# The down projection of a decoder step, with each 128-row product made as two 64-row products in two banks

## The reference

```python
def conv_ffn(x, g, w_up_l, cw, w_down_l, prev):
    u = rmsnorm(x, g) @ w_up_l
    u, new = causal_dwconv(u, prev, cw)
    a, b = jnp.split(u, 2, axis=-1)
    return (jax.nn.silu(a) * b) @ w_down_l, new      # added to x by the caller
```

## Time and profile before

| what | us |
|---|---|
| median of 3 runs | 956.81 (956.18 to 958.14) |
| the profiled execution's own time | 958.85 |
| its span, first to last instruction | 957.2 |

### The profile page before, as it was taken

The page is one execution under the profiler, slowest core; times in us unless marked ns, Lnnn a source line. Parts: engine busy times, 40 slices in busy tenths (PEclk is TensorE's granted clock), DMA queues, the critical chain, the costliest instruction groups (busy, mean ns, idle before and its releaser), DMA issues.

```text
span 957.2 us, 17553 instructions
## 1 busy us (share of the span) xinstructions
PE 915.7 (96%) x6566; PEld 860.2 (90%) x6566; DVE 627.3 (66%) x1280; ACT 446.6 (47%) x752; POOL 283.6 (30%) x565
## 2 busy tenths in 40 slices
PE   5889999998999999999989999999899999999996
PEld 4889998996779999999989999899677999999996
DVE  4667863654368999984555787355435899998442
ACT  4453541444447555553344254235444655555342
POOL 1412310252004666630042231005210465563001
PEclk9989998899789999999999999889978999999999
DMA  8654631196235566555556554108641655564432
GB/s 255 175 140 135 182 94 46 56 244 181 73 88 150 160 176 168 156 174 169 157 149 168 170 172 122 45 21 225 184 126 46 175 167 153 167 177 158 160 124 67
DMA packets 209406, 137.69 MB, mean 144 GB/s; under 512 B 23475, under 2 KB 202203, under 8 KB 209323
## 3 DMA queue, kind: packets, MB, share of 16 engines
q1 hardware_dynamic: 199904, 111.11, 41.1%
q0 software_dynamic: 8288, 22.85, 8.3%
q10 hardware_dynamic: 1131, 2.62, 0.8%
HBM read 131.11 MB, written 5.44 MB: 143 GB/s over the span
## 4 chain that ended last, share of the span: by engine, by line
PE 91%; DVE 4%; DMA 2%; ACT 1%; issue 1%; DVEq 1%; ACTq 0%; SPq 0%
PE banks L1213 22%; PE banks L1215 21%; PE banks L1214 21%; PE banks L1391 3%; PE banks L1473 2%; PE banks L1356 2%; PE banks L1441 2%; PE banks L1313 2%; PE banks L1208 2%; PE banks L1307 1%; PE banks L1369 1%; PE banks L1323 1%; PE banks L1481 1%; PE banks L1422 1%; DMA ring<-in_w_in 1%
## 5 line engine op out<-in xcount | busy, mean ns | idle before, releaser
L1215 PE MATMUL banks<-mix_r,ring_r 128*128 128x288 f32 x1008 | 300.3, 298 | 0.0
L1215 PEld LDWEIGHTS banks<-mix_r,ring_r 128*128 128x128 f32 x1008 | 193.6, 192 | 0.0
L1213 PE MATMUL banks<-mix_r,ring_r 128*128 128x288 f32 x480 | 151.1, 315 | 9.7 <-issue 6.4
L1214 PE MATMUL banks<-XG_r,keysT_r 128*128 128x288 f32 x384 | 113.3, 295 | 0.0
L1213 PEld LDWEIGHTS banks<-mix_r,ring_r 128*128 128x128 f32 x480 | 93.9, 196 | 16.5 <-issue 12.1
L1112 ACT CAST ring_r<-ring 128x1024 fp32r<-128x1024 f32 x60 | 62.5, 1047 | 98.3 <-DMA ring<-in_w_in 75.1
L1214 PE MATMUL banks<-XG_r,ring_r 128*128 128x288 f32 x352 | 107.4, 305 | 0.0
L1634 DVE TENSOR_TENSOR ring_r<-ring,keysT_r 128x2048 fp32r<-128x2048 f32 (+1 forms) x36 | 80.1, 2226 | 35.7 <-ACT keysT_r L1112 35.6
L1215 PE MATMUL banks<-phase_r,ring_r 128*128 128x288 f32 x352 | 103.1, 293 | 0.0
L890 POOL COPY phase<-ust 128x16 f32<-128x16 f32 x88 | 101.4, 1166 | 0.1
L1214 PE MATMUL banks<-XG_r,vals_r 128*128 128x288 f32 x320 | 94.4, 295 | 0.0
(11 more groups left out here) (297 smaller groups left out, 2141.1 us busy)
## 6 DMA issues: line engine op xcount, KB each, us to landing
ring<-in_w_up SPq DMA_DIRECT2D x88, 512.0 KB, 5.2
ring<-in_w_in SPq DMA_DIRECT2D x36, 512.0 KB, 4.1
ring<-in_w_down SPq DMA_DIRECT2D x16, 1024.0 KB, 5.3
ring<-in_w_down SPq DMA_DIRECT2D x8, 768.0 KB, 4.8
rawk<-in_cache_k POOLq DMA_DIRECT2D x32, 128.0 KB, 2.7
vals<-in_cache_v POOLq DMA_DIRECT2D x32, 128.0 KB, 2.4
ring<-in_w_in SPq DMA_DIRECT2D x16, 256.0 KB, 3.9
rawk<-in_cache_mem_k POOLq DMA_DIRECT2D x16, 256.0 KB, 4.8
```

The lines of the kernel that those rows point to most:

```text
L1213: mm(out_, hi_w, hi_x, start=start, stop=False)
L1214: mm(out_, hi_w, lo_x, start=False, stop=False)
L1215: return mm(out_, lo_w, hi_x, start=False, stop=stop)
```

## The change

Each 128-row matmul of the down projection becomes two of 64 rows: rows 0 to 63 of weight and input into one bank, rows 64 to 127 into the next bank, issued one after the other. A group now fills four banks where it filled two, and since it writes all four from the start, TensorE waits at its first step for the emptyings five, six, seven and eight fills earlier. VectorE adds both banks of a tile to X, one after the other with a drain between; what follows the add (L1551, L1540, and ScalarE's part) follows the second.

```diff
@@ layer_schedule
-        a("D", "down", m)
-        a("D", "down", m + 1)
+        for half in (0, 1, 2, 3):
+            a("D", "down", m + half // 2, half % 2)
         if m < 6:
             a("A", "ustate_out", m // 2)
@@ TensorE
                 elif step == "down":
-                    m = args[0]
-                    if m % 2:
+                    m, half = args
+                    if m % 2 or half:
                         continue
-                    pe.wait_ge(emptied[banks.before[fill - 7][0]], banks.before[fill - 7][1])
+                    for ahead in (5, 6, 7):
+                        w_, count = banks.before[fill - ahead]
+                        pe.wait_ge(emptied[w_], count)
                     for c3, (k0, k1) in enumerate(DOWN_K):
                         hi_w, lo_w = parts_of(l, "down", m // 2 * 3 + c3)
                         pe.wait_ge(s["h_lo"], FT * l + k1)
                         for i in (0, 1):
+                            c = slice(P * i, P * i + P)
                             for k in range(k0, k1):
-                                c = slice(P * i, P * i + P)
-                                last = split_product(ps[:, (fill + i) % 8, 0:N], hi_w[:, k - k0, c], lo_w[:, k - k0, c],
-                                                     hT_hi[:, k], hT_lo[:, k], k == 0, k == FT - 1)
-                            if k1 == FT:
-                                last.then_inc(filled, 1)
+                                for t, (w, x) in enumerate(((hi_w, hT_hi), (hi_w, hT_lo), (lo_w, hT_hi))):
+                                    for half in (0, 1):
+                                        r = slice(64 * half, 64 * half + 64)
+                                        last = mm(ps[:, (fill + 2 * i + half) % 8, 0:N], w[r, k - k0, c], x[r, k],
+                                                  start=(k, t) == (0, 0), stop=(k, t) == (FT - 1, 2))
+                                        if (k, t) == (FT - 1, 2):
+                                            last.then_inc(filled, 1)
@@ VectorE
-            def residual(l, step, m):
-                b_ = put(l, step, m)
+            def residual(l, step, m, half=1):
+                b_ = put(l, step, m, *(half,) * (step == "down"))
+                if step == "down" and half:
+                    drain()
                 v.tensor_tensor(X[:, m], X[:, m], b_[:, 0:N], ALU.add).then_inc(emptied["D"], 1)
+                if not half:
+                    return
```

More of the change, by code:

```diff
@@ L644, in last_use @@
             if kind == "down":
-                return fill_no(l, "down", i // 3 * 2 + 1)
+                return fill_no(l, "down", i // 3 * 2 + 1, 1)
             raise ValueError(kind)
@@ L899, in _ @@
                                    u[:, 258:306].rearrange("p (b x) -> p b x", x=6)[:, :, 4:6]).then_inc(s["u_last"], 1)
-                elif (step, args) == ("down", (0,)) and l + 1 < DEPTH:
+                elif (step, args) == ("down", (0, 0)) and l + 1 < DEPTH:
                     pe_done(pool, l, "up", FT - 1, 1)
@@ L937, in gained @@
                 if stage == 3:
-                    wait_emptied(act, l, "down", k)
+                    wait_emptied(act, l, "down", k, 1)
                 elif l == 0 and stage == 0:
                     wait_emptied(act, -1, "turn_x", k)
-                else:
-                    before = (l, ("", "out", "xo")[stage]) if stage else (l - 1, "down")
-                    wait_emptied(act, *before, k)
+                elif stage == 0:
+                    wait_emptied(act, l - 1, "down", k, 1)
+                else:
+                    wait_emptied(act, l, ("", "out", "xo")[stage], k)
                 c = R_FINAL + k if stage == 3 else par_col((R_MIX, R_XATTN, R_FFN)[stage], l, k)
@@ L952, in square @@
             def square(l, step, k):
-                wait_emptied(act, l, step, k)
+                wait_emptied(act, l, step, k, *(1,) * (step == "down"))
                 if k >= 2:
@@ L1087, in _ @@
                     square(l, step, args[0])
-                elif step == "down":
+                elif step == "down" and args[1]:
                     if l + 1 < DEPTH:
@@ L1102, in _ @@
                         elif l and i == 2:
-                            pe_done(act, l - 1, "down", 7)
+                            pe_done(act, l - 1, "down", 7, 1)
                         act.wait_ge(piece_in[i % 4], piece_count[l, i])
@@ L1850, in _ @@
                 elif step in ("out", "xo", "down"):
-                    residual(l, step, args[0])
+                    residual(l, step, *args)
                 elif step == "xq":
```

## The result

The changed kernel takes 990.9 us (median of 4 runs, 989.3 to 994.4) where the kernel before takes 957.5 (median of 4, one more than at the time of the forecast). The ratio is 1.0345, with a 95% interval of 1.0323 to 1.0366. The forecast was 991, with a range of 972 to 1006. The profiled execution took 992.27 us with a span of 990.6, which is compared with the 957.2 of before.

A forecast was written before the change was run, and what follows sets the result against it. TensorE was taken as the bound, busy 915.7 of 957.2 us. Pauses 22.5, clock 9.3, row changes 1.3 and adds 0.7 sum to 33.8 us more, giving 991 against the median of 956.81; range 972 to 1006.

The forecast's parts named there:

- Pairs: Down projection: 1056 pairs of 64-row matmuls, halves side by side, each pair taking one matmul's 0.131 us.
- The six pauses: Group boundaries: TensorE waits for VectorE's add behind the third chunk's rest; six at 3.75 us, 22.5 us.
- The clock: After each of six pauses TensorE falls to half clock, losing 1.55 us each, 9.3 us; bounds 0 and 18.6.
- Changes of rows, adds, ends: Switches between 128-row and 64-row work, 1.3 us; VectorE's extra adds and drains at the layers' ends, 0.7 us.
- The halves one after the other: Rival, down projection: a pair takes 0.262 us and the pause is gone; 1097 us, 9%.
- The pause without the fall of the clock: Rival, group boundaries: pauses come but the clock holds; 981 us, within the forecast's range, no separate chance given.

The follow-up runs named there:

- one half: The first run with the second half's matmuls left out except each tile's last: 962.4 us, ratio 1.0033 to the kernel before.
- the same rows: The first run with both matmuls of a pair on rows 0 to 63: 1102.4 us, ratio 1.1491 to the kernel before.
- the wait alone: Kernel before, whole matmuls, plus one wait: a group starts only after VectorE added the first tile of the group before; 993.0 us, ratio 1.0362.
- the first run: Changed kernel with VectorE's adds of a group put ahead of the rest of the next group's third chunk: 960.3 us, ratio 1.0018 to the kernel before.
- The filled pauses: Changed kernel with 22 extra matmuls, results overwritten, in each of the six pauses: 980.9 us, ratio 1.0226 to the kernel before.
- three and three: The first run, but per row tile three matmuls of rows 0 to 63, then three of rows 64 to 127: 961.0 us, ratio 1.0032.
- the run with blocks: The first run, but per chunk and tile all 24 or 18 matmuls of one half, then of the other: 1063.2 us, ratio 1.1081.

## Why the prediction was right, point by point

- **Pairs.** Taken at one matmul's 0.131 us: right. 264 matmuls in the time of 132, and the runs with one half and with the same rows bound it from both sides (0 and 142 us).
- **The six pauses.** Taken as 22.5 us: 20.9. The place, the chain and the count were right. Five boundaries lengthened by 3.1 to 3.4 us and one by 5.0. The usual one is shorter than forecast by some 0.5 us, since the third chunk now came 435.47 - 431.13 = 4.3 us after its issue and not 4.8; the last is longer, as its chunk's load took 6.1 us, and the add came later. In the run with the wait alone the load takes 434.48 - 429.65 = 4.8 us again, and its boundary grew by 3.8 us, which is the forecast's figure. Why the load is shorter in the changed kernel no run shows.
- **The clock.** Taken as six falls of 1.55 us, 9.3: right in size, not in count, and the size in part by luck. The forecast expected a fall each time since the idle times would be 3.4 us, longer than those it had seen; they were 2.8 to 3.0 us, and 4.7 once. Four of six pauses were followed by the half clock, two of them for longer than forecast within the group:

```profile
439.20:442.60 3.40, 3.40 (x52) 3.40 (x54) 1.69 (x4) 2.88 (x6) 0.00 (x0) 1.00 0.36 124
461.50:464.80 3.30, 3.30 (x31) 3.30 (x30) 1.79 (x5) 2.72 (x5) 0.00 (x0) 0.50 0.00 0
482.65:488.70 6.05, 6.05 (x50) 6.05 (x52) 3.04 (x7) 2.10 (x5) 2.16 (x5) 0.50 0.44 101
```

  The groups grew by 8.8 us; the first run's two layers of groups are longer than before by 0.6 us without any fall, which leaves 8.2 for the clock. The filled pauses give 10 us by themselves. One reading of the forecast was too short: after the 2.04 us of idle time ahead of 231.68 the clock stayed 1.00 only to the end of the stretch shown; in the next one it fell, with TensorE idle for a third of it:

```profile
233.50:237.00 3.50, 2.38 (x7) 1.38 (x7) 2.40 (x7) 2.97 (x9) 3.25 (x8) 0.67 1.19 293
```

- **Changes of rows, adds, ends.** Taken as 2.0 us together: the run without pauses measures 1.7, with an interval of 0.4 to 3.2. The split was not quite right: in that run each boundary is 0.29 us longer where 0.13 was counted, and in the changed kernel the changes of rows lie beside the pause. The tail at the end grew by 0.5, as forecast:

```profile
978.61 0.44 DVE X L1564
979.05 0.05 DVEq L1563
979.10 0.04 issue
979.14 0.46 DVE X L1564
```

  Here the second add and its drain stand in the chain, where one add stood.
- **What the sum left out.** 3.2 us of the profiled execution lie in stages that the change does not touch; its terms were 22.5 + 9.3 + 2.0 = 33.8, and those measured are 20.9 + 8.8 + 0.5 = 30.2. So the forecast's closeness owes some 3 us to chance. The four runs of the changed kernel lie 5 us apart, and the stages that the change does not touch vary by more than 3 us from trace to trace. What makes these 3 us was not shown by a run.
- **Rivals.** The halves one after the other did not happen here, but cost what was worked out when forced. The pause without the fall of the clock was made by hand and took 980.9, against 981 worked out.

## What to carry to other kernels

Before more banks are given to a group of matmuls, count the fills from one group to the next: where the wait moves from eight fills back to five, it asks for a bank that the group just before has filled, and what counts is what stands ahead of its emptying on the emptying engine, here a subtraction that waits for a load. The remedy is the order of that engine's work (the add ahead of the rest that waits), and by itself it costs nothing (ratio 0.9998). And a pause on TensorE can cost more than its length: here 8 to 10 us of half clock on 21 us of pauses. Splitting a product over the rows gave nothing by itself here, since two halves side by side took as long as the whole.

## What the runs showed of the hardware that I had not expected

- The length of an idle time alone doesn't tell whether the clock falls. In the run with the wait alone it stayed after 3.55 us and fell after 3.10 us (the groups behind the two are at 1.00 and 0.91):

```profile
461.45 0.37 PE L1213 MATMUL banks<-phase_r,keysT_r 128*128 128x288 f32 x1 [3.55 <-DVE X L1558]
461.45:478.70 17.25, 17.25 (x131) 17.25 (x132) 6.50 (x7) 5.75 (x7) 0.00 (x0) 1.00 0.35 116
...
929.67 0.37 PE L1213 MATMUL banks<-phase_r,keysT_r 128*128 128x288 f32 x1 [3.10 <-DVE X L1558]
929.67:948.60 18.93, 18.93 (x131) 18.93 (x132) 5.75 (x5) 5.74 (x7) 0.00 (x0) 0.91 0.36 115
```

  Ahead of the second piece of hq in layer 1 TensorE is idle for 2.79 or 2.80 us in the traces of all ten kernels that don't fill it. In seven of them the clock is at 0.50 within 1.5 us after the restart; in three (the first run, the wait alone, three and three) it stays 1.00. Nor does a fall come at a fixed point of the restart. In the changed kernel:

```profile
460.15 0.53 PE L1506 MATMUL banks<-phase_r,keysT_r 64*128 64x288 f32 x4 [2.82 <-DVE X L1564]
...
461.41 0.71 PE L1506 MATMUL banks<-phase_r,keysT_r 64*128 64x288 f32 x4
...
482.65 0.85 PE L1506 MATMUL banks<-phase_r,vals_r 64*128 64x288 f32 x4 [2.83 <-DVE X L1564]
```

  At 460.15 two pairs still take 0.53 us, from 461.41 on 0.71; at 482.65 they are slow from the start (0.85).
- How far TensorE went ahead in the program for the other rows: 24 matmuls on one half of the rows and then 24 on the other overlap only at the change, and take 103 us more than one and one. A group lasts 30.1 us, with the same rows 34.9, alternating 17.3 to 17.4. So by an estimate some (34.9 - 30.1) / 0.131 = 37 of 132 overlapped, at eleven changes of rows, between three and four at each, and three and three overlap wholly. The first group of the run with blocks:

```profile
415.25:445.35 30.10, 30.10 (x265) 30.10 (x264) 14.48 (x20) 7.73 (x9) 2.64 (x6) 1.00 0.36 114
```
